# One copy of the filter network's weights, its first layer ahead of the setup transposes

## What is computed

```python
z = jnp.concatenate([t, jnp.cos(bands * wpos), -jnp.sin(bands * wpos)], axis=-1)   # (seq, 33)
h = jnp.sin(z @ p['hy_f_w1'] + p['hy_f_b1'])                                       # 33 -> 64
h = jnp.sin(h @ p['hy_f_w2'] + p['hy_f_b2'])                                       # 64 -> 64
h = (h @ p['hy_f_w3'] + p['hy_f_b3']).reshape(seq_len, HY_ORDER, 2, HY_WIDTH)      # 64 -> 2 x 2 x 512
window = jnp.exp(-t[:, :, None, None] * jnp.abs(p['hy_decay'])) + HY_MOD_SHIFT
h = h * window
h = h * lax.rsqrt(jnp.sum(h * h, axis=(0, 2), keepdims=True) + EPS)
```

## Time and profile before

| | |
|---|---|
| median of three runs | 835.96 us |
| time of the profiled execution | 835.31 us |
| its span (first to last instruction) | 833.5 us |
| PE busy | 781.1 us, 94% of the span |
| VectorE (DVE), ScalarE (ACT), POOL busy | 50%, 33%, 13% |
| the chain that ended last | PE 77%, DMA 8%, DVE 6%, issue 3%, ACT 3% |
| HBM | 173.66 MB read, 16.45 MB written, 228 GB/s over the span |

### The profile page before, as it was taken

One profiled execution on the slowest core, in us unless ns is written; L12 is line 12 of the kernel. 1 busy time (PEld: TensorE's weight loads), 2 busy tenths in 40 slices (PEclk: granted clock), 3 DMA queues, 4 the chain that ended last, 5 costly groups with the idle time before them and its releaser, 6 DMA issues.

```text
span 833.5 us, 16953 instructions
## 1 busy us (share of the span) xinstructions
PE 781.1 (94%) x6753; PEld 447.1 (54%) x6753; DVE 418.0 (50%) x763; ACT 277.8 (33%) x558; POOL 108.4 (13%) x213
## 2 busy tenths in 40 slices
PE   3999899999999998999999998599999999899975
PEld 1232455554554456456664454267777777566632
DVE  3766712225881694855555685733333333233327
ACT  1767611114100302256232243123333333233325
POOL 4000100000001000001002000122222222122231
PEclk9999999999999999999999999799999999999989
DMA  7988442032053603034009506899999999999337
GB/s 247 412 332 328 146 195 74 28 127 75 4 198 137 171 1 126 3 127 127 1 24 408 192 41 254 310 389 413 421 419 416 414 420 420 419 415 416 116 108 290
DMA packets 40709, 190.92 MB, mean 229 GB/s; under 512 B 4761, under 2 KB 5125, under 8 KB 33037
## 3 DMA queue, kind: packets, MB, share of 16 engines
q1 hardware_dynamic: 29256, 154.60, 46.8%
q0 software_dynamic: 8640, 29.00, 10.0%
q10 hardware_dynamic: 2758, 6.52, 2.2%
HBM read 173.66 MB, written 16.45 MB: 228 GB/s over the span
## 4 chain that ended last, share of the span: by engine, by line
PE 77%; DMA 8%; DVE 6%; issue 3%; ACT 3%; POOL 1%; ACTq 0%; POOLq 0%; SPq 0%; DVEq 0%
PE banks L2059 17%; PE banks L1712 17%; PE banks L2072 8%; PE banks L1850 4%; PE banks L1713 4%; DMA arena<-in_w_up 4%; PE banks L1859 4%; PE banks L1954 3%; PE banks L1944 2%; DMA arena<-in_x_sample 2%; PE banks L1657 2%; PE banks L1609 2%; PE banks L1744 2%; PE banks L1679 1%; PE banks L1912 1%
## 5 line engine op out<-in xcount | busy, mean ns | idle before, releaser
L2059 PE MATMUL banks<-arena 128*32 128x256 f32 x3072 | 176.8, 381 | 5.0 <-DMA arena<-in_w_up 3.9
L1712 PE MATMUL banks<-arena 128*128 128x512 f32 x320 | 164.2, 595 | 1.5 <-issue 0.8
L2059 PEld LDWEIGHTS banks<-arena 128*32 128x32 f32 x3072 | 115.4, 111 | 58.1 <-issue 6.8
L1713 PEld LDWEIGHTS banks<-arena 128*128 128x128 f32 x320 | 60.8, 190 | 76.5 <-issue 76.5
L1515 DVE STREAM_TRANSPOSE arena<-arena 128x256 f32<-128x256 f32 x49 | 32.2, 657 | 127.9 <-PE banks L2059 127.4
L2072 PE MATMUL banks<-arena 128*32 128x256 f32 x1536 | 92.7, 379 | 1.2 <-DVE arena L1539 1.2
L2072 PEld LDWEIGHTS banks<-arena 128*32 128x32 f32 x1536 | 57.4, 110 | 26.8 <-DVE arena L1539 1.7
L1713 PE MATMUL banks<-arena 128*128 128x128 f32 x320 | 61.5, 274 | 0.0
L917 ACT ACTIVATE arena<-banks 32x256 f32<-32x256 f32 x98 | 36.7, 374 | 71.3 <-PE banks L2072 70.7
L1522 DVE COPY arena<-banks 32x256 f32<-32x256 f32 x98 | 41.4, 422 | 33.5 <-PE banks L2072 32.8
L1712 PEld LDWEIGHTS banks<-arena 128*128 128x128 f32 x320 | 48.6, 192 | 4.8 <-issue 3.3
(11 more groups left out here) (387 smaller groups left out, 985.2 us busy)
## 6 DMA issues: line engine op xcount, KB each, us to landing
arena<-in_w_down SPq DMA_DIRECT2D x16, 2048.0 KB, 28.6
arena<-in_w_gate SPq DMA_DIRECT2D x15, 2048.0 KB, 24.5
arena<-in_w_up SPq DMA_DIRECT2D x15, 2048.0 KB, 29.9
arena<-in_w_ada SPq DMA_DIRECT2D x12, 2048.0 KB, 11.4
arena<-in_w_in SPq DMA_DIRECT2D x7, 2048.0 KB, 7.8
expert_output<-arena ACTq DMA_DIRECT2D x49, 128.0 KB, 6.4
expert_output<-arena POOLq DMA_DIRECT2D x1, 4096.0 KB, 20.4
arena<-in_w_out SPq DMA_DIRECT2D x2, 2048.0 KB, 8.0
```

The source lines that it names most:

```text
L1712: M(ps[:, b, :], lhs, hT[:, k, CTX:TOK], start=k == 0, stop=k == KD - 1)
L1713: mm = M(ps[:, b + 1, 0:CTX], lhs, hT[:, k, 0:CTX], start=k == 0, stop=k == KD - 1)
L2059: mm = M(ps[q * LANE:(q + 1) * LANE, 2, 0:2 * P].rearrange("p (g a j) -> p g a j", g=2, j=LANE), xg[:, k, :], gate_up[e % 3][:, :, k, q, : ...
```

## The change

- The features stand in 34 partitions x 640. Layer 1 has one copy of its weights (`w1sb`, 34 x 64) and runs as two matmuls, one for each half of the tokens, each to its half of the output partitions. It waits for three loads (`ld_mlp` at 48), all on SP's queue, and stands ahead of the setup transposes on PE.
- Layer 2 has its weights twice, one below the other (`w2pair`, 128 x 64), and runs as two matmuls as well. Its two weight loads and two bias loads are all on SP's queue and count on a new semaphore, `ld_layer2`.
- No tile needs zeroes any more: two memsets of POOL go, and the counts of `ones_ready` are lower by two.
- VectorE turns the decays into rates behind both layers, for both orders in a row. The copy of `colsT` moves behind layer 1's argument.
- The warm-up matmuls read `hid1`, 320 columns, and no longer wait for the rates.
- The adaptive pieces of order 0 stand after w = 5, 7 and 9 in place of 3, 6 and 9.
- The semaphore `y_zeroed` is merged into `out_stored` (80 in place of 64 and 16).

```diff
     feats = np.concatenate([np.concatenate(feats, axis=0).T, np.ones((1, TOK))], axis=0)
-    out["features"] = np.concatenate([feats[:, 0:HALF], feats[:, HALF:TOK]], axis=0)
+    out["features"] = feats
     cols = np.zeros((P, 8))
...
     neg_decay = area(W3, 4 * MW)
-    feat = area(W3 + 2048, HALF, rows=2 * (FE + 1))
+    feat = area(W3 + 2048, TOK, rows=FE + 1)
     hid1 = area(W3 + 2688, HALF)
...
     qtmp = area(W5 + 640, HALF)
-    w1pair = area(W5 + HALF, 2 * FH, rows=2 * (FE + 1))
-    w2pair = area(W5 + HALF + 2 * FH, 2 * FH)
+    w1sb = area(W5 + HALF, FH, rows=FE + 1)
+    w2pair = area(W5 + HALF + FH, FH)
     hy_bias_row = area(W5, ORD, MW, rows=1)
...
         sp.dma_start(feat, a["features"]).then_inc(S["ld_mlp"], 16)
-        sp.wait_ge(S["ones_ready"], 2)
-        sp.dma_start(w1pair[0:FE, 0:FH], a["hy_f_w1"][0]).then_inc(S["ld_mlp"], 16)
-        sp.dma_start(w1pair[FE:FE + 1, 0:FH], a["hy_f_b1"]).then_inc(S["ld_mlp"], 16)
-        sp.dma_start(w2pair[0:FH, 0:FH], a["hy_f_w2"][0]).then_inc(S["ld_mlp"], 16)
-        sp.dma_start(b2col[0:FH, :], a["hy_f_b2"][0].rearrange("(n o) -> n o", o=1)).then_inc(S["ld_mlp"], 16)
+        sp.dma_start(w1sb[0:FE, :], a["hy_f_w1"][0]).then_inc(S["ld_mlp"], 16)
+        sp.dma_start(w1sb[FE:FE + 1, :], a["hy_f_b1"]).then_inc(S["ld_mlp"], 16)
+        sp.dma_start(w2pair[0:FH, :], a["hy_f_w2"][0]).then_inc(S["ld_layer2"], 16)
+        sp.dma_start(w2pair[FH:2 * FH, :], a["hy_f_w2"][0]).then_inc(S["ld_layer2"], 16)
+        for half in range(2):
+            sp.dma_start(b2col[half * FH:(half + 1) * FH, :], a["hy_f_b2"][0].rearrange("(n o) -> n o", o=1))\
+                .then_inc(S["ld_layer2"], 16)
         sp.dma_start(w3e[0:FH, :], a["hy_f_w3"][0]).then_inc(S["ld_w3"], 16)
...
         link = linker(pool, "pool_chain")
-        link(pool.memset(w1pair, 0.0), "ones_ready")
-        link(pool.memset(w2pair, 0.0), "ones_ready")
         link(pool.memset(cpad, 0.0), "ones_ready")
...
         pool.dma_start(y_dram[last - KD * P:last, :].rearrange("(p t) (k c) -> p (t k) c", p=P, c=P),
-                       zeros.unsqueeze(1).broadcast_to((P, KD * KD, P))).then_inc(S["y_zeroed"], 16)
+                       zeros.unsqueeze(1).broadcast_to((P, KD * KD, P))).then_inc(S["out_stored"], 16)
         pool.wait_ge(S["iv_read"], 5)
...
         pool.wait_ge(S["st_ready"], 8)
-        pool.wait_ge(S["out_stored"], 64)
-        pool.wait_ge(S["y_zeroed"], 16)
+        pool.wait_ge(S["out_stored"], 80)
         for i in range(3):
...
             act.dma_start(rows1[row:row + n, :], src).then_inc(S["ld_setup"], 16)
-            if row == 0:
-                act.wait_ge(S["ones_ready"], 2)
-                act.dma_start(w1pair[FE + 1:2 * FE + 1, FH:2 * FH], a["hy_f_w1"][0]).then_inc(S["ld_mlp"], 16)
-                act.dma_start(w1pair[2 * FE + 1:2 * FE + 2, FH:2 * FH], a["hy_f_b1"]).then_inc(S["ld_mlp"], 16)
         act.dma_start(rows2[0:KD, :], a["c_ctx"].rearrange("(k p) -> k p", p=P)).then_inc(S["ld_setup"], 16)
...
 
-        act.dma_start(w2pair[FH:2 * FH, FH:2 * FH], a["hy_f_w2"][0]).then_inc(S["ld_mlp"], 16)
-        act.dma_start(b2col[FH:2 * FH, :], a["hy_f_b2"][0].rearrange("(n o) -> n o", o=1)).then_inc(S["ld_mlp"], 16)
 
         act.wait_ge(S["setup_t"], 2)
-        act.wait_ge(S["ones_ready"], 3)
+        act.wait_ge(S["ones_ready"], 1)
         link(A(cpad[:, :, 0:2].rearrange("p k g -> p g k"), ps[:, 7, 0:16].rearrange("p (g k) -> p g k", g=2), ACT.Silu),
...
         link(A(hid1, ytmp, ACT.Sin), "hid_ready")
-        act.wait_ge(S["ones_ready"], 7)
-        act.wait_ge(S["arg_ready"], 3)
+        act.wait_ge(S["ones_ready"], 5)
+        act.wait_ge(S["arg_ready"], 2)
         for half in range(2):
...
                 act.wait_ge(S["filt_read"], 14 * ((w - 2) // 10) + (w - 2) % 10 + 1)
-            act.wait_ge(S["arg_ready"], 2 + 2 * o)
+            act.wait_ge(S["arg_ready"], 3 + o)
             c = (2 * o + s) * MW
...
 
-        dve.wait_ge(S["setup_t"], 1)
-        link(CP(colsT, ps[:, 0, 0:120]), "cols_ready")
         for layer in range(2):
...
             link(TS(ytmp, ytmp, PI, -PI, ALU.min, ALU.max), "arg_ready")
-            dve.wait_ge(S["ld_w3"], 64)
-            rates = neg_decay[:, layer * D:(layer + 1) * D]
+            if layer == 0:
+                dve.wait_ge(S["setup_t"], 1)
+                link(CP(colsT, ps[:, 0, 0:120]), "cols_ready")
+        dve.wait_ge(S["ld_w3"], 64)
+        for o in range(ORD):
+            rates = neg_decay[:, o * D:(o + 1) * D]
             link(STT(rates, rates, -1.0, rates, ALU.mult, ALU.min), "arg_ready")
...
         link(dve.tensor_reduce(gate_fold, ident.rearrange("p (s c) -> p c s", c=LANE), AX_X, ALU.add))
-        dve.wait_ge(S["ones_ready"], 7)
+        dve.wait_ge(S["ones_ready"], 5)
         folded = gate_fold[:, 0:4 * H].rearrange("p (g h) -> p g h", h=H)
...
 
+        pe.wait_ge(S["ld_mlp"], 48)
+        for half in range(2):
+            mm = M(ps[half * FH:(half + 1) * FH, 1, 0:HALF], w1sb, feat[:, half * HALF:(half + 1) * HALF], start=True, stop=True)
+        mm.then_inc(S["mlp_done"], 1)
         pe.wait_ge(S["ld_setup"], 112)
...
         pe.transpose(ps[:, 7, 0:16], rows2, ident[0:16, 0:16]).then_inc(S["setup_t"], 1)
-
-        pe.wait_ge(S["ld_mlp"], 144)
-        for layer, (w, x) in enumerate(((w1pair, feat), (w2pair, hid1))):
-            if layer:
-                pe.wait_ge(S["hid_ready"], 1)
-            M(ps[:, 1 + 2 * layer, 0:HALF], w, x, start=True, stop=True).then_inc(S["mlp_done"], 1)
-        pe.wait_ge(S["ones_ready"], 7)
+        pe.wait_ge(S["ld_layer2"], 64)
+        pe.wait_ge(S["hid_ready"], 1)
+        for half in range(2):
+            rows = slice(half * FH, (half + 1) * FH)
+            mm = M(ps[rows, 3, 0:HALF], w2pair[rows, :], hid1[rows, :], start=True, stop=True)
+        mm.then_inc(S["mlp_done"], 1)
+        pe.wait_ge(S["ones_ready"], 5)
         pe.wait_ge(S["cols_ready"], 1)
...
         pe.wait_ge(S["ld_w3"], 64)
-        pe.wait_ge(S["arg_ready"], 2)
         for _ in range(WARM):
-            M(ps[:, 5, :], ident, neg_decay[:, 0:MW], start=True, stop=True)
+            M(ps[:, 5, 0:HALF], ident, hid1, start=True, stop=True)
         pe.wait_ge(S["hid_ready"], 2)
...
                     sum_squares(o, 0 if w == 5 else 1)
-                piece = ((3, 6, 9), (3, 6, 9))[o]
+                piece = ((5, 7, 9), (3, 6, 9))[o]
                 if w in piece:
```

More of the change, by code:

```diff
@@ L302, in emit @@
     h2_quarters = h2_dram.rearrange("t (q c) -> (t q) c", q=LANES)
-    names = """ld_setup ld_mlp ld_w3 ld_hybias ld_dft ld_x ld_late ld_gate ld_state ld_rowctx ld_rowlat
-        ld_x2 ld_route ld_gr2 rows_stored y_zeroed out_stored  all_stored
+    names = """ld_setup ld_mlp ld_layer2 ld_w3 ld_hybias ld_dft ld_x ld_late ld_gate ld_state ld_rowctx ld_rowlat
+        ld_x2 ld_route ld_gr2 rows_stored out_stored  all_stored
         ada_done ada_row ada_t mod_ready setup_t cols_ready cvec_ready mlp_done arg_ready hid_ready ones_ready x_rstd xn_ready
```

## The result

| | before | changed |
|---|---|---|
| median, us | 836.1 (16 runs, 833.34 to 838.38) | 839.29 (16 runs, 837.35 to 840.76) |
| profiled execution: span, us | 833.5 | 838.7 |

The ratio is 1.0036, with a 95% interval of 1.0026 to 1.0046: slower by 3.0 us. The forecast was no measurable change (836.1); the measured median lies above its range (834.2 to 837.7).

What follows compares the result with a forecast made beforehand. Bound by the chain from the small filter-network loads to the filters, beside loads keeping the DMA engines full from 20 to 45 us. Sum -0.48 + 0.6 = +0.1 us on the 835.96 median: 836.1 us, range 834.2 to 837.7.

Steps and rivals of the forecast that it cites:

- Loads of the filter network and the layers: Head of the kernel: three loads instead of nine start layer 1 at 6.3 us (11.19 before), layer 2 at 10.7.
- Filters at 15.5: First filter matmul on PE at 15.5 us instead of 20.49, a lead of 5.0 us.
- the cover of the warm-up's shortening: Warm-up before the filters: a low clock costs the first four up to 3 us, hidden behind the late adaptive slot.
- Adaptive pieces: Order-0 pieces after filters 5, 7, 9: same PE work reordered, PE waits 2.2 us or more for the third slot.
- d: Delay of the slots' and x's landing from SP's extra issues: 0.6 us taken, -0.4 to +2.0 possible.
- What of the lead arrives, 0.48 - d: At transform group 7: of the 3.7 us lead only 0.48 - d gets through, because x lands at 44.9 + d.
- the gate: Group 7 waits for VectorE's bank read, which follows x's landing: released at 53.15 + d, starting 53.42 + d.
- Rival C: Slower by the clock: PE pauses drop it to half rate behind group 7, 837.8 up to 838.7 us; chance 0.12.
- Its first pause: PE stands still before the third adaptive piece for 2.2 us + d, which only eats lead.
- its second: PE idle before group 7, some 3 us; a clock fall there costs 2.6 us, or 1.7 if it rises after four passes.
- the 0.8 estimated by that page: Features in 34 rows use 2 engines, not 4: 0.8 us longer on engines 0 and 1; not used in the sum.

Runs made afterwards that it cites:

- b_pieces: Kernel before with only the order-0 adaptive pieces moved to after filters 5, 7 and 9; ratio to before 1.0002.
- a_pieces: Changed kernel with the order-0 adaptive pieces after filters 3, 6 and 9 again; ratio to before 1.0016.
- a_nowarm: Changed kernel without its two warm-up matmuls; ratio to before 1.0007.
- w4_queue: a_warm4 with the second copies of layer 2's weight and bias on ScalarE's queue again; ratio to before 1.0014.
- a_warm4: Changed kernel with four warm-up matmuls of 320 columns in place of two, no longer waiting for the decays; 837.18 us, ratio to before 1.0007.
- combo: a_warm4 and a_xearly together; ratio to before 0.9991.
- a_xearly: Changed kernel with the loads of x right behind the third slot, ahead of the wait for the first adaptive piece; median 838.05 us, ratio to before 1.0007.
- best: combo with w4_queue's queues, transform matrices loaded behind the third slot, fourth adaptive piece behind transform group 6 instead of 3; 832.58 us, ratio to before 0.9952.

## Why the prediction was wrong

- **Loads of the filter network and the layers**: right. Layer 1 at 5.92 (6.3 forecast, 5.2 to 8.1), layer 2 at 10.26 (10.7), each 1.33 us (1.43), the first product at 18.53 (18.4).
- **Filters at 15.5**: 1.0 us too early. I let the warm-up run from 12.1, but it still waits for the decays, and these land at 14.1. Their own wait was in the diff; I had asked when the signs are ready and not when the decays arrive.
- **The step that failed is the cover of the warm-up's shortening.** I wrote "the first four filters would be up to 3 us longer", and "What is late then is the adaptive slot below, so that too is hidden". The low clock didn't end after four filters: it lasted up to the first adaptive piece and through most of it. From the first filter to the end of the second sum of squares it took 20.5 us (16.53 to 37.06) and not 14.7. The slot, which landed at 33.9, was passed unseen (PE came to it at 38.05), so it covered nothing. The same edit alone on the kernel before costs 0.47%. A longer warm-up on the changed kernel brings the filter passes to 0.43 and the time to 1.0007. Leaving the warm-up out gives the same time with the passes at 0.85. So the times show that the short warm-up is the bad one, and the traces how it costs.
- **Adaptive pieces**: by themselves free, as priced (b_pieces). With the low clock they put the first full-height work two filters later (a_pieces: passes of 0.43 from 27.2, not 30.2).
- **d**: third slot at 33.9, so 0.5 (0.6 taken). x was 2.9 late, and that was no term of mine. How much of it is the stretch in which the loads ran dry stays open: x was 1.7 late in a_pieces, where they didn't run dry, and 0.1 late in a_nowarm. The share of the extra issues on SP stays open too: with them the third slot lands at 33.5 to 34.4 in nine traces, with the queue as before at 33.0 to 33.6 in four. (The windows from 20 to 45 us reach 105%, not the 104 that I wrote.)
- **What of the lead arrives, 0.48 - d**: the gate is there, where the filters are fast. With x 0.25 us late in w4_queue group 7 starts at 53.41 (53.42 + 0.25 forecast) and the first product stands at 58.59 (58.5 + 0.25), with x 1.3 late in a_warm4 at 54.50 (54.75) and 59.68 (59.83). In the changed kernel, which had no lead to lose, the gate only added the 0.37 us.
- **Rival C** had the right cause, the clock, in the wrong place: I asked when it would fall again and not whether it rises at all. Its first pause is real, but only in kernels whose filters are fast (a_warm4, w4_queue, combo, a_xearly); behind its second, 1.39 us in w4_queue, passes stay at 0.43.
- **Size.** The profile of the changed kernel is 2.24 us late at the first product of order 1, its second trace 1.27; the medians differ by 3.2. The rest lies behind, where single traces of all these kernels differ by up to 7.6 us from that mark to the end of the span (771.3 to 778.9). Whether a part of it belongs to the change stays open: the merged semaphore of the output stores acts there, and no run has it alone.

The Trainium skill was cited for rival C ("TensorE: Matmul & The Clock Gate", "HAM oscillation — how this bites in real kernels") with the rule that a wait for data can put PE back to half rate; a_warm4 bears it out, with a granted clock of 0.50 behind a pause of 3.25 us. On the spread of a load over engines ("DMA: Bandwidth & Descriptors", "Why a DMA increments its semaphore by 16 and not by 1") no run has the features alone. In w4_queue, with the features in 34 rows and as many loads on SP's queue as before, the third slot lands 0.2 to 0.7 us later than in the three traces with 68 rows, which differ by 0.5 among themselves; the 0.8 estimated by that page is neither shown nor excluded.

## What to carry to other kernels

Read the pace of one repeated matmul, start to start, before you call dummy work free: 0.85 us against 0.43 for the same pass says at which level the array is, and the rows ahead of the change say what brought it up. Whoever edits a warm-up should keep its height and length and see what it waits for, or try the kernel without it; and when a chain is made earlier, list what else has to have arrived by then (a slot, the tokens, the decays), for each of these is the next bound and each pause for one can cost the clock.

## What the runs showed of the hardware

- Unbroken filter passes on 65 of 128 rows left TensorE at 1.2 GHz in seven traces: twelve passes in 10.4 to 10.6 us in five of them, eight in 7.0 to 7.2 us in two. Eight warm-up records on 128 rows (3.59 to 4.63 us) stood before 2.4 GHz in four traces, the same on 65 rows (4.63 us) before 1.2 in one. Four of 320 columns on 128 rows (2.3 to 2.5 us) stood before 1.2 GHz in four traces and before 2.4 in one. Once risen, the clock held through the same 65-row passes (12 in 5.66 us).
- Behind pauses of PE of 2.2 us (a_xearly), 2.9 (w4_queue), 3.25 (a_warm4) and 3.3 (combo) the adaptive piece took 3.0 to 3.6 us in place of 1.92. Behind one of 1.5 us (best) the passes stayed at 0.43.
- The granted clock of the windows reads 1.00 over the first 30 us of the changed kernel, while its filter passes come at half pace. It shows 0.50 for a fall later on (a_warm4, 35 to 40). Before the first rise the pace of the passes is the one to trust.
- Two matmuls on separate halves of the output partitions took 1.33 us in four records, less than one of full width in two (1.43).
